# A fused two-block transformer layer on one core: modulation weights loaded first, two modulation blocks ahead of the squares of x, and the context normed during the Fourier projection

## The chip, the cores and the metric

The kernel runs on one core of a Trainium2 chip. The core has a matrix engine (TensorE, PE), a vector engine (VectorE, DVE), a scalar engine (ScalarE, ACT), a small general engine (GpSimd, POOL) and SyncE (SP), which here issues all DMAs in one queue. Each engine executes its own list of instructions in order and waits on semaphores that others raise. The metric is the time of the program on the device in microseconds (us), lower being better.

## The reference

A diffusion-style block with a context (depth 1) and then two layers of a second block. All data is float32, sequence 512, width 1024, context length 256. What matters here is the start:

```python
mod  = silu(c)     @ w_mod + b_mod          # c: one row; w_mod: 1024 x 6144
modc = silu(c_ctx) @ w_mod + b_mod
sh1, sc1, g1, sh2, sc2, g2 = split(mod, 6)  # the same for modc
h  = rms(x,  norm1) * (1 + sc1)  + sh1      # x:  512 x 1024
hc = rms(xc, norm1) * (1 + csc1) + csh1     # xc: 256 x 1024
P  = project(h)                             # h @ w_in: Fourier part, q, k, v, delta-rule inputs, gates
Pc = project(hc)                            # the context needs k, v, delta-rule inputs and gates, not the Fourier part
...                                         # attention, delta rule both ways, Fourier mix, w_out, MLP, then block 2 twice
```

rms(x, g) divides each row by the root of its mean square, and multiplies by g.

## The kernel before

Activations lie transposed: partition = channel within a tile of 128, free dimension = token. x is XT (8 tiles of 128 x 512), the context is XC (8 tiles of 128 x 256). A dense product takes its weights in pieces of 4 x 128 rows and 256 columns (512 KB, RAW). Each piece is split in two parts (SPL, "hi" by ACT at L1714, "lo" by DVE at L1998), and the product is made as three matmuls of parts (L1346); the activations are split likewise (HS for x, HC for the context, each with hi and lo). RAW and SPL have four slots.

The start of the program has these steps:

- SP issues the small constants, XT, XC, eight modulation pieces (MW, 512 KB each, into eight slots), the first four dense pieces (Fourier columns in two pieces, gates in a small one, and one more), small constants, and then, each when its slot has been used, modulation pieces 8 to 15.
- `mean_square` (L421): ACT squares a tile into one of three TMP slots, PE adds its column sums by a matmul with ones (L1381), DVE makes mean + eps (L2023), ACT the root (L1731), DVE the reciprocal (L2026). The result is R for x and RC for the context.
- `mod(j)` (L349): eight matmul groups over two pieces (L1361) make 256 columns of the modulation for c and c_ctx as a row; DVE copies it to MR (L2004, three buffers); two small matmuls turn it to columns (L1372); DVE adds the bias into MOD (L2008). mod(j) for j = 0 to 3 holds shifts, for 4 to 7 scales.
- After each pair of modulation blocks `gain` makes SCG = g (1 + scale), and `modulate` makes two tiles of HS: DVE x * SCG * R into TMP (L2041), ACT adds the shift and writes hi (L1735), DVE writes lo (L2046). `modulate` emits the DVE step of the next tile ahead of the lo step of the tile before it, if it is called for more than one tile.
- `split_first` stands in the plan ahead of the third pair: there ACT and DVE split the first four dense pieces (L1255 to L1264 of the planner).
- `dense(W["w_in"][0] ...)` is the Fourier projection (48 matmuls of 128 x 512), then come the gates (24 matmuls of 16 x 256 on HC, 24 of 16 x 512 on HS) and the projections that both x and the context need.

The order of each engine's list is that of the plan (`emit`). Work that is to lie beside dense matmuls is written as a generator in a list (`behind`, `aside`); `products` calls `tick` after each group of matmuls, and each tick lets each generator do one step. With rate 2 there are two ticks for each group. PSUM banks are handed out in turn (`single`, `pair`).

## Time and profile before

| | |
|---|---|
| time, median of 3 runs | 3332.59 us (3331.94 to 3334.54) |
| the profiled execution's own time | 3333.74 us |
| its span, first to last instruction | 3331.9 us |
| PE busy | 3178.4 us, 95% of the span |
| DVE, ACT busy | 1773.2 us (53%), 1112.9 us (33%) |
| mean granted TensorE clock | 0.969 |
| DMA | 288.19 MB, mean 86 GB/s |

The profile is of one execution. Its times are counted from the first instruction. PE is close to always busy after the first tenth, but not at the start: in the page's first slice of 83 us it is busy for seven tenths, with the granted clock at 0.8 of full speed, and the DMA queue moves 243 GB/s there against 86 on average. The granted clock has two levels, 0.50 (1.2 GHz) and 1.00 (2.4 GHz); a value between is a mean over a stretch. An instruction is shown with its line of the kernel, what it writes and reads, and, in brackets, how long its engine was idle in front of it and who ended the wait. A matmul in plain float32 is recorded as two, a matmul of split parts as one. The modulation weights appear as MW, and SP's own issue instructions as SPq.

### The profile page before, as it was taken

Reading aid. Unit: us, or ns where it says so; the run is one execution under the profiler, and the core shown is the slowest. Engines: PE = TensorE matmul, PEld = TensorE weight load, DVE = VectorE, ACT = ScalarE, POOL = GpSimd, SP = SyncE. Lnnn points to the kernel's source line nnn. Section 1 sums busy time; section 2 is a strip of 40 time slices with the busy share of each in tenths; the row PEclk is TensorE's granted clock in tenths of the full one; section 3 lists DMA queues with packets and bytes.
Section 4 is the critical chain, followed back from the end, with each engine's and each line's share of the span. In section 5 each row is a group of like instructions: output and inputs, shape, how many; then the busy total and the mean of one; then the engine's idle time right before and its main releaser. Section 6 shows DMA issues by size and latency. Waiting matters only on the chain.

```text
span 3331.9 us, 42705 instructions
## 1 busy us (share of the span) xinstructions
PE 3178.4 (95%) x17856; PEld 2509.2 (75%) x17856; DVE 1773.2 (53%) x2414; ACT 1112.9 (33%) x1574; POOL 63.3 (2%) x65
## 2 busy tenths in 40 slices
PE   7796889989999999999999999999999999999997
PEld 4564864578888888876788888888887767888886
DVE  4534554353435434587865434654345877643446
ACT  3321224342333322334443223432233254432233
POOL 0001410000000000000000000000000000000000
PEclk8897987999999999999999999999999999999999
DMA  6231000123222222221122322323222212223222
GB/s 243 93 119 51 4 32 1 38 77 101 95 95 101 95 95 98 91 99 45 64 101 90 101 96 91 104 100 97 99 88 88 89 45 89 89 101 97 93 91 73
DMA packets 81935, 288.19 MB, mean 86 GB/s; under 512 B 9552, under 2 KB 11344, under 8 KB 81360
## 3 DMA queue, kind: packets, MB, share of 16 engines
q1 hardware_dynamic: 81744, 285.46, 25.7%
q8 instruction: 142, 2.33, 0.3%
q14 instruction: 49, 0.40, 0.0%
HBM read 283.33 MB, written 2.10 MB: 86 GB/s over the span
## 4 chain that ended last, share of the span: by engine, by line
PE 90%; DVE 5%; issue 3%; ACT 1%; DMA 1%; POOL 0%; SPq 0%; DVEq 0%; ACTq 0%; POOLq 0%
PE PS L1346 77%; PE PS L1428 3%; PE PS L1663 1%; PE PS L1607 1%; PE PS L1627 1%; PE PS L1665 1%; PE PS L1361 1%; DVE XD L2114 1%; PE PS L1615 1%; PE PS L1684 1%; DMA MW<-in_w_mod 1%; PE PS L1673 1%; DVE SM L2290 1%; PE PS L1557 0%; ACT SPL L1714 0%
## 5 line engine op out<-in xcount | busy, mean ns | idle before, releaser
L1346 PE MATMUL PS<-HS,SPL 128*128 128x512 f32 (+1 forms) x7752 | 1804.9, 393 | 10.0 <-DVE HS L2046 7.3
L1346 PEld LDWEIGHTS PS<-HS,SPL 128*128 128x128 f32 (+1 forms) x7752 | 1455.2, 188 | 331.3 <-issue 20.7
L1998 DVE TENSOR_TENSOR SPL<-RAW,SPL 128x1024 fp32r<-128x1024 f32 (+1 forms) x491 | 584.2, 1193 | 722.5 <-ACT SPL L1714 718.8
L1714 ACT ACTIVATE SPL<-RAW 128x1024 fp32r<-128x1024 f32 (+1 forms) x491 | 503.2, 1028 | 843.7 <-PE PS L1346 843.4
L1346 PE MATMUL PS<-FF,SPL 128*128 128x512 f32 x2880 | 654.6, 389 | 0.0
L1346 PEld LDWEIGHTS PS<-FF,SPL 128*128 128x128 f32 x2880 | 540.6, 188 | 112.2
L2375 DVE SCALAR_TENSOR_TENSOR CA<-AP__137,CW,CA 128x512 f32<-128x512 f32 x240 | 180.1, 750 | 6.2
L1899 ACT ACTIVATE FF<-TMP 128x512 fp32r<-128x512 f32 x88 | 55.7, 633 | 235.1 <-DVE TMP L2345 235.1
L1893 ACT ACTIVATE SA<-SA 128x512 f32<-128x512 f32 x88 | 55.6, 633 | 191.4 <-DVE SA L2335 191.4
L2335 DVE TENSOR_TENSOR SA<-PS,R 128x512 f32<-128x512 f32 x88 | 60.5, 692 | 98.5 <-PE PS L1346 98.2
L2290 DVE TENSOR_REDUCE SM<-PS 128x1 f32<-128x768 f32 (+2 forms) x96 | 61.8, 644 | 87.3 <-PE PS L1608 50.3
L1842 ACT ACTIVATE PB<-PS,SM 128x768 f32<-128x768 f32 (+2 forms) x96 | 62.7, 653 | 110.1 <-DVE SM L2290 109.4
L2347 DVE TENSOR_TENSOR FF<-TMP,FF 128x512 fp32r<-128x512 f32 x88 | 61.0, 693 | 66.1 <-ACT FF L1899 66.1
L1346 PE MATMUL PS<-MS,SPL 128*128 128x512 f32 x384 | 88.0, 390 | 1.2 <-DVE MS L2460 1.2
L1346 PEld LDWEIGHTS PS<-MS,SPL 128*128 128x128 f32 x384 | 71.9, 188 | 16.9 <-DVE MS L2460 2.0
L2311 DVE SCALAR_TENSOR_TENSOR HS<-XT,VEC,HS 128x512 fp32r<-128x512 f32 x64 | 48.1, 752 | 55.8 <-ACT HS L1878 49.0
L2316 DVE SCALAR_TENSOR_TENSOR XT<-PS,XT 128x512 f32<-128x512 f32 x80 | 55.1, 689 | 40.0 <-PE PS L1346 40.0
L1878 ACT ACTIVATE HS<-XT,VEC 128x512 fp32r<-128x512 f32 x56 | 40.6, 724 | 96.1 <-DVE XT L2316 96.1
L2342 DVE TENSOR_TENSOR TMP<-PS,R 128x512 f32<-128x512 f32 x88 | 60.5, 688 | 21.6 <-PE PS L1346 21.6
L2345 DVE TENSOR_TENSOR TMP<-TMP,SA 128x512 f32<-128x512 f32 x88 | 60.9, 693 | 3.0
L1721 ACT ACTIVATE TMP<-XT 128x512 f32<-128x512 f32 x80 | 49.5, 619 | 33.6 <-DVE XT L2316 17.9
L2019 DVE TENSOR_TENSOR ACC<-ACC,TMP 128x512 f32<-128x512 f32 x76 | 52.2, 687 | 10.4 <-ACT TMP L1721 9.8
(289 smaller groups left out, 2258.6 us busy)
## 6 DMA issues: line engine op xcount, KB each, us to landing
RAW<-in_w_ff_in SPq DMA_DIRECT2D x176, 512.0 KB, 3.7
RAW<-in_w_in SPq DMA_DIRECT2D x88, 512.0 KB, 3.7
RAW<-in_w_ff_out SPq DMA_DIRECT2D x80, 512.0 KB, 3.5
RAW<-in_w_ff SPq DMA_DIRECT2D x64, 512.0 KB, 3.6
MW<-in_w_mod SPq DMA_DIRECT2D x48, 512.0 KB, 4.7
RAW<-in_w_out SPq DMA_DIRECT2D x24, 512.0 KB, 3.7
RAW<-in_w_ple_gate SPq DMA_DIRECT2D x16, 512.0 KB, 3.7
RAW<-in_w_ff_out SPq DMA_DIRECT2D x16, 256.0 KB, 2.7
```

The source lines that it names most:

```text
L1346: m = pe.matmul(o, w[x][:, k, rows], r.T[:, r.k0 + k, y, 0:r.cols], start=r.start and k == 0 and (x, y) == (0, 0), stop=r.stop and k == r. ...
L1428: m = pe.matmul(PS[hp, o.b, 64 * x:64 * x + 64], lhs[h][:, x, :], rhs[h][:, x, :] if len(rhs[h].shape) == 3 else rhs[h], start=True, stop= ...
L1714: a.activation(SPL[:, s, 0, 0:n], RAW[:, s, 0:n], AF.Copy).then_inc(w_hi, 1)
L1842: a.activation(s.row[:, 0:s.n], two_banks(s.uses, s.n), AF.Exp, bias=s.stat[:, 0:1], accum_out=s.stat[:, 1:2]).then_inc(free[s.uses[0].b], 1)
L1899: a.activation(FF[:, r.k, 0, :], TMP[:, r.slot, :], AF.Copy).then_inc(s_ffhi, 1)
L1998: v.tensor_tensor(SPL[:, s, 1, 0:n], RAW[:, s, 0:n], SPL[:, s, 0, 0:n], ALU.subtract).then_inc(w_lo, 1)
L2290: v.tensor_reduce(s.stat[:, 0:1], two_banks(s.uses, s.n), AX, ALU.max, negate=True).then_inc(s_mx, 1)
L2335: v.tensor_tensor(SA[:, r.sa, :], PS[:, r.use.b, :], R[:, :], ALU.mult).then_inc(free[r.use.b], 1)
L2342: v.tensor_tensor(t, PS[:, r.use.b, :], R[:, :], ALU.mult).then_inc(free[r.use.b], 1)
L2345: v.tensor_tensor(t, t, SA[:, r.sa, :], ALU.mult).then_inc(s_glu, 1)
L2347: v.tensor_tensor(FF[:, r.k, 1, :], t, FF[:, r.k, 0, :], ALU.subtract).then_inc(s_fflo, 1)
L2375: m = v.scalar_tensor_tensor(out=acc, in0=x, scalar=w, in1=acc, op0=ALU.mult, op1=ALU.add)
```

## The change

SP no longer issues XC directly behind XT. Behind XT come modulation pieces 0 to 7 and only the first dense piece; dense pieces 1 to 3, XC and the small constants are issued where modulation piece 7 has been used, behind the fetch of piece 15. The squares of x are emitted behind the first two modulation blocks. The squares of the context, RC and the eight HC tiles are a generator in `behind`, which runs during the Fourier projection, one `modulate` call for each tile. What is left of it behind the projection is drained there.

```diff
@@ -436,8 +436,6 @@
         give(u)
         return r.done
 
-    m_r = mean_square(XT, m_x, R[:, :], 512)
-    m_rc = mean_square(XC, m_xc, RC[:, :], 256)
 
     def gain(at, name, j, n, waits):
         r = Rec()
@@ -468,16 +466,39 @@
         if k < 4:
             mod(k)
             mod(4 + k)
-        else:
+        if k == 0:
+            m_r = mean_square(XT, m_x, R[:, :], 512)
+        if k == 4:
             tick()
         if k:
             i = 2 * k - 2
             gain(8, "n1", i, 2, [mod_mark[k - 1], mod_mark[3 + k]])
             hx_ready += modulate(HS, (i, i + 1), lambda j: XT[:, j, :], lambda j: SCG[:, j, 0:1],
                                  lambda j: MOD[:, j, 0:1], R[:, :], 512, [m_r])
-    hc_ready = modulate(HC, range(8), lambda j: XC[:, j, :], lambda j: SCG[:, j, 1:2], lambda j: MOD[:, j, 1:2],
-                        RC[:, :], 256, [m_rc])
     catch_up()
+    hc_ready = []
+
+    def context():
+        u = single()
+        for j in range(8):
+            r = Rec()
+            r.x, r.mark, r.use, r.j, r.n = XC[:, j, :], m_xc, u, j, 256
+            r.slot, r.after = tmp()
+            r.sq = count(s_sq)
+            slot_end[r.slot] = r.added = count(s_part) if j < 7 else u.mark
+            emit("square_sum", r)
+            if j % 2:
+                yield 1
+        r = Rec()
+        r.use, r.dst, r.n, r.width = u, RC[:, :], 256, 1024
+        r.root, m_rc = count(s_root), count(s_rms)
+        emit("root_of", r)
+        give(u)
+        for j in range(8):
+            hc_ready.extend(modulate(HC, (j,), lambda j: XC[:, j, :], lambda j: SCG[:, j, 1:2],
+                                     lambda j: MOD[:, j, 1:2], RC[:, :], 256, [m_rc]))
+            if j % 2:
+                yield 1
 
     ev_marks, qk_done = {}, {}
     apart.append(mods_apart(range(8, 24)))
@@ -493,7 +514,10 @@
         return ev
 
     rate[0] = 2
+    behind.append(context())
     dense(W["w_in"][0], 8, HS, hx_ready, evac_to(FT, 0, "f"))
+    while behind:
+        tick()
 
 
     m_tri = load("tri", TRI[:, :, :], D["c_tri"])
@@ -1286,15 +1310,9 @@
         sp.dma_start(ones[:, :], D["c_ones"]).then_inc(landed["ones"], 16)
         sp.dma_start(ident[:, :], D["c_ident"]).then_inc(landed["id"], 16)
         sp.dma_start(XT[:, :, :], D["xT"]).then_inc(landed["x"], 16)
-        sp.dma_start(XC[:, :, :], D["ctxT"]).then_inc(landed["xc"], 16)
         for p in mod_pieces[:8]:
             fetch_mod(p)
-        for p in pieces[:4]:
-            fetch(p)
-        sp.dma_start(onesbd[:, :], D["c_onesbd"]).then_inc(landed["bd"], 16)
-        sp.dma_start(idb[:, :], D["c_idb"]).then_inc(landed["idb"], 16)
-        sp.dma_start(causal[:, :], D["c_causal"]).then_inc(landed["causal"], 16)
-        sp.dma_start(madd[:, :, :], D["c_madd"]).then_inc(landed["madd"], 16)
+        fetch(pieces[0])
 
         def split(p):
             if p.i + 4 < len(pieces):
@@ -1306,6 +1324,14 @@
                 sp.wait_ge(*r.used)
                 fetch_mod(r.p.then)
             if r.p.i == 7:
+                fetch(pieces[1])
+                sp.dma_start(XC[:, :, :], D["ctxT"]).then_inc(landed["xc"], 16)
+                for p in pieces[2:4]:
+                    fetch(p)
+                sp.dma_start(onesbd[:, :], D["c_onesbd"]).then_inc(landed["bd"], 16)
+                sp.dma_start(idb[:, :], D["c_idb"]).then_inc(landed["idb"], 16)
+                sp.dma_start(causal[:, :], D["c_causal"]).then_inc(landed["causal"], 16)
+                sp.dma_start(madd[:, :, :], D["c_madd"]).then_inc(landed["madd"], 16)
                 for p in mod_pieces[16:18]:
                     fetch_mod(p)
```

SP's list at its start, before. MW_69 are the modulation slots of pieces 0 to 15, MW those of later pieces, RAW the dense weights (w_in, w_gates):

```order
4 L1288 DMA XT<-in_xT 128x4096
5 L1289 DMA XC<-in_ctxT 128x2048
6 L1283 DMA MW_69<-in_w_mod 128x1024 x8
7 L1280 DMA RAW<-in_w_in 128x1024 x2
8 L1280 DMA RAW<-in_w_gates 128x128
9 L1280 DMA RAW<-in_w_in 128x1024
10 L1294 DMA onesbd<-in_c_onesbd 128x128
11 L1295 DMA idb<-in_c_idb 128x128
12 L1296 DMA causal<-in_c_causal 128x128
13 L1297 DMA madd<-in_c_madd 128x128
14 L1283 DMA MW_69<-in_w_mod 128x1024 x8
15 L1283 DMA MW<-in_w_mod 128x1024 x2
```

And with the change:

```order
4 L1312 DMA XT<-in_xT 128x4096
5 L1307 DMA MW_69<-in_w_mod 128x1024 x8
6 L1304 DMA RAW<-in_w_in 128x1024
7 L1307 DMA MW_69<-in_w_mod 128x1024 x8
8 L1304 DMA RAW<-in_w_in 128x1024
9 L1328 DMA XC<-in_ctxT 128x2048
10 L1304 DMA RAW<-in_w_gates 128x128
11 L1304 DMA RAW<-in_w_in 128x1024
12 L1331 DMA onesbd<-in_c_onesbd 128x128
13 L1332 DMA idb<-in_c_idb 128x128
14 L1333 DMA causal<-in_c_causal 128x128
15 L1334 DMA madd<-in_c_madd 128x128
```

XC (128x2048) has moved from behind XT to behind all sixteen first modulation pieces and the second dense piece; three of the four dense pieces stand there too.

PE's list from its start, before. ones is the operand of the square sums, C_66 the conditioning columns, MR a modulation row:

```order
1 L1381 MATMUL PS<-TMP,ones 128x512 x8
2 L1381 MATMUL PS<-TMP,ones 128x256 x8
3 L1361 MATMUL PS<-MW_69,C_66 32x256 x12
4 L1372 MATMUL PS<-VEC,MR 128x2 x2
5 L1361 MATMUL PS<-MW_69,C_66 32x256 x8
6 L1372 MATMUL PS<-VEC,MR 128x2 x2
```

And with the change:

```order
1 L1387 MATMUL PS<-MW_69,C_66 32x256 x12
2 L1398 MATMUL PS<-VEC,MR 128x2 x2
3 L1387 MATMUL PS<-MW_69,C_66 32x256 x4
4 L1407 MATMUL PS<-TMP,ones 128x512 x8
5 L1387 MATMUL PS<-MW_69,C_66 32x256 x4
6 L1398 MATMUL PS<-VEC,MR 128x2 x2
7 L1387 MATMUL PS<-MW_69,C_66 32x256 x8
8 L1398 MATMUL PS<-VEC,MR 128x2 x2
```

Four modulation pieces (16 matmuls) now stand ahead of the squares of x (128x512 x8), and the context's squares (128x256 x8) are gone from there. In the Fourier projection PE's list with the change is as follows, where L1372 are dense matmuls and L1407 the context's squares:

```order
19 L1372 MATMUL PS<-HS,SPL 128x512 x12
20 L1407 MATMUL PS<-TMP,ones 128x256 x4
21 L1372 MATMUL PS<-HS,SPL 128x512 x12
22 L1387 MATMUL PS<-MW,C_66 32x256 x4
23 L1407 MATMUL PS<-TMP,ones 128x256 x4
24 L1372 MATMUL PS<-HS,SPL 128x512 x24
25 L1387 MATMUL PS<-MW,C_66 32x256 x4
26 L1372 MATMUL PS<-HC,SPL 16x256 x24
```

The context's squares stand between the dense matmuls of the first and second piece; before, nothing but the two modulation pieces stood there.

DVE's list for the context, before (L2041 is the first step of a tile, L2046 its lo part):

```order
35 L2041 SCALAR_TENSOR_TENSOR TMP<-XT,SCG,R 128x512 x2
36 L2046 SCALAR_TENSOR_TENSOR HS<-TMP,MOD,HS 128x512 x2
37 L2041 SCALAR_TENSOR_TENSOR TMP<-XC,SCG,RC 128x256 x2
38 L2046 SCALAR_TENSOR_TENSOR HC<-TMP,MOD,HC 128x256
39 L2041 SCALAR_TENSOR_TENSOR TMP<-XC,SCG,RC 128x256
40 L2046 SCALAR_TENSOR_TENSOR HC<-TMP,MOD,HC 128x256
41 L2041 SCALAR_TENSOR_TENSOR TMP<-XC,SCG,RC 128x256
42 L2046 SCALAR_TENSOR_TENSOR HC<-TMP,MOD,HC 128x256
```

And with the change (L2067 and L2072 are the same two steps, L2024 the split, L2049 and L2052 make RC):

```order
34 L2072 SCALAR_TENSOR_TENSOR HS<-TMP,MOD,HS 128x512 x2
35 L2024 TENSOR_TENSOR SPL<-RAW,SPL 128x1024
36 L2049 TENSOR_SCALAR RC<-PS 128x256
37 L2052 RECIPROCAL RC<-RC 128x256
38 L2067 SCALAR_TENSOR_TENSOR TMP<-XC,SCG,RC 128x256
39 L2072 SCALAR_TENSOR_TENSOR HC<-TMP,MOD,HC 128x256
40 L2067 SCALAR_TENSOR_TENSOR TMP<-XC,SCG,RC 128x256
41 L2072 SCALAR_TENSOR_TENSOR HC<-TMP,MOD,HC 128x256
42 L2067 SCALAR_TENSOR_TENSOR TMP<-XC,SCG,RC 128x256
43 L2072 SCALAR_TENSOR_TENSOR HC<-TMP,MOD,HC 128x256
44 L2067 SCALAR_TENSOR_TENSOR TMP<-XC,SCG,RC 128x256
```

The split of the fifth dense piece and RC stand ahead of the HC tiles, and the two steps of a tile follow each other, where before the next tile's first step stood between them. The first four splits stand where they stood: behind the first HS pair and ahead of the third modulation pair.

## Rows read from the trace of the kernel before

**Rows 1.** Page, section 4 (chain by engine) and two groups of section 5.
```profile
PE 90%; DVE 5%; issue 3%; ACT 1%; DMA 1%; POOL 0%; SPq 0%; DVEq 0%; ACTq 0%; POOLq 0%
...
L1998 DVE TENSOR_TENSOR SPL<-RAW,SPL 128x1024 fp32r<-128x1024 f32 (+1 forms) x491 | 584.2, 1193 | 722.5 <-ACT SPL L1714 718.8
L1714 ACT ACTIVATE SPL<-RAW 128x1024 fp32r<-128x1024 f32 (+1 forms) x491 | 503.2, 1028 | 843.7 <-PE PS L1346 843.4
```

**Rows 2.** All engines by stretch: busy us, granted clock, DMA share, GB/s.
```profile
0.00:10.00 10.00, 0.00 (x0) 0.00 (x0) 0.23 (x1) 1.50 (x2) 0.52 (x5) 1.00 0.79 287
10.00:20.00 10.00, 9.07 (x16) 3.81 (x16) 0.00 (x0) 6.10 (x9) 0.00 (x0) 1.00 1.00 386
36.00:47.00 11.00, 5.49 (x40) 3.03 (x40) 8.60 (x15) 4.79 (x7) 0.00 (x0) 0.65 1.02 414
```

**Rows 3.** Chain of waits, in order of time: start us, length us, what.
```profile
2.12 8.02 DMA XT<-in_xT
...
28.91 0.61 PE PS L1372 x4
29.51 0.61 PE PS L1361 x8
30.15 0.44 DVE MR L2004
...
34.01 0.16 DVE SCG L2031
```

**Rows 4.** Timeline of PE: start us, us, line op out<-in xcount [idle before].
```profile
10.93 9.34 PE L1381 MATMUL PS<-TMP,ones 128*128 128x512 f32 x16 [10.93 <-ACT TMP L1727]
22.11 3.76 PE L1381 MATMUL PS<-TMP,ones 128*128 128x256 f32 x16 [1.84 <-ACT TMP L1727]
...
41.51 1.01 PE L1372 MATMUL PS<-VEC,MR 128*128 128x2 f32 x4 [5.75 <-DVE MR L2004]
42.45 1.93 PE L1361 MATMUL PS<-MW,C 128*32 128x256 f32 x16
...
51.12 8.20 PE L1346 MATMUL PS<-HS,SPL 128*128 128x512 f32 x24
...
59.82 5.74 PE L1346 MATMUL PS<-HS,SPL 128*128 128x512 f32 x24
...
66.80 2.96 PE L1346 MATMUL PS<-HC,SPL 128*16 128x256 f32 x24 [0.66 <-issue]
```

**Rows 5.** Timeline of DVE.
```profile
21.70 3.35 DVE L2026 RECIPROCAL R<-R 128x512 f32<-128x512 f32 x1 [0.69 <-ACT R L1731]
...
37.35 3.70 DVE L1998 TENSOR_TENSOR SPL<-RAW,SPL 128x1024 fp32r<-128x1024 f32 x4 [0.19 <-ACT SPL L1714]
...
56.51 0.87 DVE L2041 SCALAR_TENSOR_TENSOR TMP<-XC,SCG,RC 128x256 f32<-128x256 f32 x2
...
61.93 0.48 DVE L2041 SCALAR_TENSOR_TENSOR TMP<-XC,SCG,RC 128x256 f32<-128x256 f32 x1
...
62.99 0.48 DVE L2046 SCALAR_TENSOR_TENSOR HC<-TMP,MOD,HC 128x256 fp32r<-128x256 f32 x1 [0.18 <-ACT HC L1735]
```

**Rows 6.** PE by stretch: length, busy us (x), granted clock, DMA share, GB/s.
```profile
25.00:36.00 11.00, 8.74 (x108) 1.00 0.89 301
36.00:39.00 3.00, 0.00 (x0) 1.00 1.03 414
42.00:56.00 14.00, 12.96 (x67) 0.50 0.40 158
88.00:94.00 6.00, 5.41 (x16) 0.50 0.00 0
304.00:309.00 5.00, 2.60 (x73) 1.00 0.00 0
309.00:310.00 1.00, 1.00 (x26) 0.50 0.00 0
```

**Rows 7.** Landing times of the modulation weights' DMAs up to 70 us.
```profile
DMA to landing us min/median/max: 3.7/8.6/16.4
```

## The prediction

> **What bounds the kernel now.** I read the page first. The chain that ended last is 90% TensorE (PE) [rows 1], and the change touches only the first 90 us, so the question is how many microseconds later or sooner PE gets through that stretch; everything behind it waits on PE, VectorE (DVE) and ScalarE (ACT) and moves along with it. Then I read the stretch in stages, in the order in which the prediction uses them.
>
> The DMA queue is full from the start: 287 GB/s in the first 10 us, 386 in the next, 414 from 36 to 47 [rows 2]. x lands at 10.14 [rows 3]. PE then does the squares of x, 10.93 to 20.27, and those of the context, 22.11 to 25.87 [rows 4]. R is finished by DVE at 25.05 and RC at 28.57 (25.87 plus 2.70; its reciprocal is the 1.75 in front of the first copy of a modulation row) [rows 5]. Rounds of PE and DVE follow [rows 3], and then DVE reaches the four splits of w_in, 37.35 to 41.05 [rows 5]. From their end it takes 10.07 us to the first dense matmul at 51.12 [rows 4]; I call that start t0. While DVE splits PE is idle, 5.75 us [rows 4], and its granted clock falls: 1.00 (2.4 GHz) at 36 to 39, 0.50 (1.2 GHz) from 42 to 56 [rows 6]. The Fourier projection's 24+24 matmuls end at about 65.6, the gates' matmuls on HC run 66.80 to 69.76 [rows 4]: HC was complete at 63.47 [rows 5], so PE hardly waits for it. The last HC triplet ends 69.76-51.12 = 18.6 us after t0.
>
> **Front: where t0 goes.** The change takes the context's 1.05 MB and 1.3 MB of dense weights and constants from ahead of the last eight modulation pieces. But the split of the first four dense pieces keeps its place on DVE, ahead of the third modulation pair, and it needs pieces 1, 2 and 3, which now are asked for only behind modulation piece 15, with the context between them. So I work out both arrivals.
>
> DVE's arrival at the splits. Four modulation pieces must now land and be used before the squares of x. Bytes up to piece 3: 0.30 of vectors, 2.10 of x, 4x0.524, together 4.50 MB; x landed when 2.87 MB had moved against 2.40 of its own, so 0.47 more are in flight: 4.97 MB, at 386 GB/s from 2.87 at 10 us: 15.4 us. Its matmuls, at the lower clock about 1.0 us: 16.4. Squares of x 9.34 [rows 4] (I take that their first third runs at half the pace of the rest, as now: the modulation matmuls ahead of them are no help, since the same mix from 42 on, 1.93 us for two pieces, did not raise the clock before the dense matmuls had run for 5 us [rows 4, 6]): 25.7. To R finished 25.05-20.27 = 4.78: 30.5. DVE has been shut behind that reciprocal; then MR 0.44, PE 0.61 for the columns and 0.61 for piece 7, MR 0.44 [rows 3], and 0.2 for the handovers: 32.8. From SCG to the splits 37.35-34.01 = 3.34 [rows 3, 5]: 36.1, which is 1.2 before today's. So of the 6.5 us from 22.11 to 28.57 that the context takes on the chain, the wait for four pieces ahead of the squares of x gives back most.
>
> Arrival of the weights. Piece 15 may be fetched when piece 7 is used, which stands behind the MR copy: 32.3. A 512 KB piece needs at least 3.7 us to land [rows 7]: 36.1. Behind it dense piece 1, the context, the gates' weights and dense piece 3, 0.524+1.049+0.066+0.524 = 2.16 MB at 414 GB/s: 5.2, so 41.3. ACT's half of the split 1.03, DVE's 1.19 [rows 1], two handovers of 0.1: 43.7 against 41.05 (the gates' piece fits in between). Behind the waiting splits on DVE stand the MR copies of the third pair, and PE waits for these. t0 is **2.7 us later**. Bounds: had the queue never paused, the 13.47 MB up to dense piece 3 and 0.4 in flight would be through at 10+11.0/0.40 = 37.5, and the splits end at 39.9, t0 1.2 earlier; with 1.5 us more for the small constants or a slower landing it is 4.2 later. I take 2.7, since the refetch of a slot needs PE's use of it, and that is in the order.
> The queue here moves 414 GB/s [rows 2]. The Trainium skill (DMA: Bandwidth & Descriptors, Where 436 GB/s comes from) gives about 358 GB/s as what HBM grants one core. By it even the unbroken stream would end at 40.7 and the early case would vanish; the row of this case decides.
>
> **Context beside the Fourier projection.** Counted from t0. First 12 matmuls at the lower clock 5.1 (12 of the 24 in 8.20; the other 12 take 3.1) [rows 4]. Four squares of the context: half of 3.76, so 1.9; ACT can make them in time, since DVE is done with HS at 56.51, +5.4 [rows 5], and ACT before it. 12 matmuls 3.1, a modulation piece 0.6, four squares 1.9: +12.6. RC 2.7, handover 0.1: +15.4. Then the eight HC tiles. Today DVE issues the next TMP before it asks ACT for the last tile, and a tile costs 0.77 (56.51 to 61.93, seven steps) [rows 5]. The new loop calls modulate for one tile at a time, and the order shows TMP, HC, TMP, HC in strict turn. One tile alone is TMP at 61.93, ACT, then HC from 62.99 to 63.47: 1.54, and as DVE starts the next instruction 0.08 before the one in front ends, 1.46. Eight tiles 11.7, one MR copy between them 0.35: HC is complete at +27.4, its last three matmuls end at +27.8.
> PE meanwhile: second half of the projection 5.7 and a modulation piece 0.6 [rows 4], so it stands at the gates' matmuls at +18.9 and waits there, doing three matmuls (0.37) for each tile. **27.8-18.6 = 9.2 us lost**. Of it 3.8 is the squares, which now lie on PE inside the projection, the rest is the wait. Bounds: 3.8 if the tiles ran at today's 0.77 after all (5.4 less than 9.2), 10.7 if the first squares still meet the lower clock. I take 9.2, from the order.
> The FT copies and the next split on ACT now stand behind the eight HC activations; ACT is through with HC at about +26.9; two FT copies of 0.6, the split's 1.03 and 1.19 on DVE end at +30.9. PE needs that split behind the gates' 24 matmuls on x (512 columns, 5.7 like the half projection), at +33.5, so these hide it; without them it would add 3 us. POOL's pad memsets wait for the last HC tile too; nothing needs them before XD's sums.
>
> **Clock.** From +18.9 to +27.8 PE is busy about a quarter of the time. At 304 to 309 it was busy 2.60 of 5 us and the clock fell right behind, 0.50 at 309 [rows 6]. So I expect a fall during the wait, and the stretch 88 to 94 [rows 6] shows what one costs: some 5.4 us of PE's work at half speed, **2.6 us** lost. Bounds 0 (it holds) and 7.1 (24 gates' matmuls of 16 columns all at 0.43 instead of 0.24, 4.5, and another 2.6 behind them). I take the ordinary stretch.
> The Trainium skill (TensorE: Matmul & The Clock Gate, A second HAM failure mode) says that frequent short idles between groups of matmuls can make the clock swing. The stretch before 309 bears it out; by it the 2.6 stand, without it the sum is the second rival's.
>
> **Sum.** 2.7+9.2+2.6 = 14.5 us on the profiled execution's 3333.74 (span 3331.9): 3348.2. That execution lies 1.15 above the median of the runs, so I predict **3347 us**.
>
> **Rivals.**
> 1. The clock holds in the wait. For it: from 25 to 36 PE had gap after gap and kept 1.00. Against: PE was busy 8.74 of those 11 us [rows 6]; here it would be a quarter. 2.7+9.2 = 11.9, 3344.5.
> 2. The clock falls and the thin gates' matmuls do not raise it. For it: from 42 on PE was busy with small matmuls nearly throughout, at 0.50 [rows 6]. Against: 16x512 streams without pause. 2.7+9.2+7.1 = 19.0, 3351.5.
> 3. The queue keeps up and t0 is 1.2 early. For: the bytes. Against: the refetch waits for PE. -1.2+9.2+2.6, 3343.
> 4. Not slower: in front of the third pair PE's idle is so short that its clock never falls. Needs dense pieces 1 to 3 there when DVE comes, at 33.8 if the squares of x run warm (2.5 sooner): splits end at 37.5, t0 3.5 early; and the upper clock from there saves 3.8 on the small matmuls (four column groups 1.01 against 0.61, five pieces 0.97 against 0.54) and 2.2 on the first 12 dense ones [rows 3, 4]. -9.5+9.2+2.6, 3335. It decides if PE's idle there ends while the clock is still up, as it is at 36 to 39 [rows 6]; today the idle is 5.75 [rows 4]. Against it: the byte count, which puts the weights at 37.5 at best.
>
> That the context isn't hidden, as the change has it, is the main case itself.
>
> **Chances.** Forecast 0.42, rival 1 0.18, rival 2 0.18, rival 3 0.16, rival 4 0.06. Range: the outer ends 3343 and 3351.5 widened by the bounds of t0, 3341 to 3353. What a measurement of this kernel tells from no change is about 0.2%, 6.7 us: only rival 4 (3335) falls inside it, with a little of rival 3. Faster 0.01, same 0.07, slower 0.92.
>
> **What would show it.** Splits on DVE ending at 42 to 45; XC squares inside the projection; HC tiles 1.46 apart; gates' HC matmuls stretched from 3 us to about 9, with PE idle waiting for DVE's HC; granted clock 0.50 behind. HC tiles 0.8 apart, or splits ending before 39, would break the sum; a shift at 84 us (the gate chain on ACT) that is smaller than at 70 would mean that a later wait takes some of it up.

## The result, and the profile after

| | before | after |
|---|---|---|
| median | 3333.57 us (3331.94 to 3336.30, 4 runs) | 3353.41 us (3352.90 to 3355.47, 4 runs) |
| profiled execution, span | 3333.74, 3331.9 | 3353.65, 3351.8 |

The ratio is 1.0059, 95% interval 1.0047 to 1.0071: slower, by about 20 us, where 14.5 on the profiled execution had been forecast. The time lies 0.4 us above the upper end of the range.

The page shows the same kind of program (compare [rows 1]): the chain is still PE's, and the splits of the weights and the matmuls take what they took.

```profile
PE 89%; DVE 5%; issue 3%; ACT 2%; DMA 1%; POOL 0%; SPq 0%; DVEq 0%; ACTq 0%; POOLq 0%
...
L2024 DVE TENSOR_TENSOR SPL<-RAW,SPL 128x1024 fp32r<-128x1024 f32 (+1 forms) x491 | 584.3, 1193 | 737.1 <-ACT SPL L1740 733.3
L1740 ACT ACTIVATE SPL<-RAW 128x1024 fp32r<-128x1024 f32 (+1 forms) x491 | 503.3, 1028 | 847.2 <-PE PS L1372 841.7
```

So nearly all of the 20 us must come from the first 110 us, and the table of marks below has 18.84 of it there. This is PE's timeline there (start us, us, line op out<-in xcount, and the idle before it), to be held against [rows 4]:

```profile
11.72 2.29 PE L1387 MATMUL PS<-MW,C 128*32 128x256 f32 x16 [11.72 <-DMA MW<-in_w_mod]
...
17.23 9.25 PE L1407 MATMUL PS<-TMP,ones 128*128 128x512 f32 x16
...
31.66 0.94 PE L1398 MATMUL PS<-VEC,MR 128*128 128x2 f32 x4 [3.07 <-DVE MR L2030]
...
46.79 1.02 PE L1398 MATMUL PS<-VEC,MR 128*128 128x2 f32 x4 [9.52 <-DVE MR L2030]
...
58.71 4.75 PE L1372 MATMUL PS<-HS,SPL 128*128 128x512 f32 x12 [2.16 <-issue]
63.29 1.93 PE L1407 MATMUL PS<-TMP,ones 128*128 128x256 f32 x8
...
76.48 0.52 PE L1372 MATMUL PS<-HC,SPL 128*16 128x256 f32 x3
77.57 0.52 PE L1372 MATMUL PS<-HC,SPL 128*16 128x256 f32 x3 [0.56 <-DVE HC L2072]
79.02 0.52 PE L1372 MATMUL PS<-HC,SPL 128*16 128x256 f32 x3 [0.93 <-DVE HC L2072]
80.48 0.82 PE L1372 MATMUL PS<-HC,SPL 128*16 128x256 f32 x3 [0.94 <-DVE HC L2072]
...
86.64 0.82 PE L1372 MATMUL PS<-HC,SPL 128*16 128x256 f32 x3 [0.64 <-DVE HC L2072]
87.25 6.88 PE L1372 MATMUL PS<-HS,SPL 128*16 128x512 f32 x24
```

Four things stand out. The idle in front of the third modulation pair has grown from 5.75 to 9.52 us. The first dense matmul (t0) has a wait of 2.16 of its own, which it did not have before, and comes at 58.71 instead of 51.12. The gates' matmuls on HC go in threes, each waiting for its tile. And there is a wait of 3.07 at 28.6, in which PE has nothing to do while DVE makes R.

The long idle is best read in the chain of waits (start us, us, what); before, the same stretch had no DMA in it:

```profile
31.66 0.94 PE PS L1398 x4
32.60 1.05 PE PS L1387 x8
...
33.67 0.33 SPq L1307
...
34.04 0.43 SPq L1304
...
34.52 1.20 SPq L1328
...
35.75 0.43 SPq L1304
...
36.23 7.77 DMA RAW<-in_w_in
...
44.02 1.06 ACT SPL L1740
```

SP gets to modulation piece 15 at 33.67, spends 2.56 us on asking for what stands between, asks for dense piece 3 at 36.23, and it lands at 44.00. Ahead of that request the chain is PE's: column matmuls and modulation piece 7 take 0.94 and 1.05 at the lower clock, where before they took 0.61 and 0.61 [rows 3]. DVE's four splits, a single group of 3.70 us in [rows 5], are now apart (the third, of the small gates' piece, starts at 43.01 and takes 0.29):

```profile
37.43 1.23 DVE L2024 TENSOR_TENSOR SPL<-RAW,SPL 128x1024 fp32r<-128x1024 f32 x1 [0.20 <-ACT SPL L1740]
41.02 1.23 DVE L2024 TENSOR_TENSOR SPL<-RAW,SPL 128x1024 fp32r<-128x1024 f32 x1 [2.37 <-ACT SPL L1740]
...
45.11 1.22 DVE L2024 TENSOR_TENSOR SPL<-RAW,SPL 128x1024 fp32r<-128x1024 f32 x1 [1.80 <-ACT SPL L1740]
```

PE by stretch (length, busy us (x), granted clock, DMA share, GB/s), for [rows 2, 6]:

```profile
26.00:32.00 6.00, 2.93 (x32) 0.98 0.53 172
32.00:44.00 12.00, 5.27 (x39) 0.50 0.89 313
44.00:62.00 18.00, 12.01 (x64) 0.50 0.40 160
64.00:79.00 15.00, 13.53 (x72) 1.00 0.29 95
82.00:88.00 6.00, 3.83 (x14) 0.50 0.01 1
90.00:100.00 10.00, 10.00 (x106) 1.00 0.43 149
```

The clock is down from 32 on; before it was still at 1.00 from 36 to 39 [rows 6]. And from 26 to 32 the queue moves 172 GB/s, less than half of what it can: SP stands at requests that need a slot PE has not yet used (it waits for PE seven times, 23.3 us in all, up to 60).

Marks in the two timelines, in us:

| | before | after | shift |
|---|---|---|---|
| last of the first four splits ends | 41.05 | 46.33 | +5.28 |
| from there to t0 | 10.07 | 12.38 | +2.31 |
| from t0 to the gates' matmuls on x | 18.48 | 28.54 | +10.06 |
| from there to the matmuls with TRI | 18.99 | 20.18 | +1.19 |
| matmuls with TRI | 88.59 | 107.43 | +18.84 |
| profiled execution | 3333.74 | 3353.65 | +19.91 |

The last 1.07 us come later. Behind the gate chain the clock in after is 0.54 from 134 to 136, where before it was 1.00 at the same work (114 to 116). The matmuls on XD there take longer, and the next matmuls on HC start at 141.72 instead of 120.88: the shift has grown to 20.84, of which 0.93 is gone by the end. No experiment was made on that.

### The profile page after: what moved, and what is told of

Its sections match the earlier page's. It is cut to its first block, busy times and chain, and to the rows that moved or that the text cites. A ratio compares the mean times of both kernels' runs of the same rounds, so it can differ in the third digit from the quotient of the medians.

```text
span 3351.8 us, 42704 instructions
## 1 busy us (share of the span) xinstructions
PE 3187.6 (95%) x17856; PEld 2510.6 (75%) x17856; DVE 1773.3 (53%) x2414; ACT 1112.8 (33%) x1574; POOL 63.2 (2%) x65
## 4 chain that ended last, share of the span: by engine, by line
PE 89%; DVE 5%; issue 3%; ACT 2%; DMA 1%; POOL 0%; SPq 0%; DVEq 0%; ACTq 0%; POOLq 0%
PE PS L1372 76%; PE PS L1454 3%; PE PS L1689 1%; DMA MW<-in_w_mod 1%; PE PS L1633 1%; PE PS L1653 1%; PE PS L1387 1%; PE PS L1691 1%; DVE XD L2140 1%; PE PS L1641 1%; PE PS L1710 1%; PE PS L1699 1%; DVE SM L2316 1%; ACT SPL L1740 0%; PE PS L1583 0%
## 5 line engine op out<-in xcount | busy, mean ns | idle before, releaser
L1372 PE MATMUL PS<-HS,SPL 128*128 128x512 f32 (+1 forms) x7752 | 1805.4, 393 | 12.2 <-DVE HS L2072 7.3
L1372 PEld LDWEIGHTS PS<-HS,SPL 128*128 128x128 f32 (+1 forms) x7752 | 1454.5, 188 | 334.0 <-issue 24.3
L2024 DVE TENSOR_TENSOR SPL<-RAW,SPL 128x1024 fp32r<-128x1024 f32 (+1 forms) x491 | 584.3, 1193 | 737.1 <-ACT SPL L1740 733.3
L1372 PE MATMUL PS<-FF,SPL 128*128 128x512 f32 x2880 | 654.6, 389 | 0.0
L1372 PEld LDWEIGHTS PS<-FF,SPL 128*128 128x128 f32 x2880 | 540.5, 188 | 112.3
L1372 PE MATMUL PS<-MS,SPL 128*128 128x512 f32 x384 | 88.0, 390 | 1.2 <-DVE MS L2486 1.2
L1372 PEld LDWEIGHTS PS<-MS,SPL 128*128 128x128 f32 x384 | 71.9, 188 | 16.9 <-DVE MS L2486 2.0
L1387 PE MATMUL PS<-MW,C 128*32 128x256 f32 x384 | 38.4, 491 | 23.5 <-DMA MW<-in_w_mod 23.4
```

What stands on the lines that cost most here:

```text
L1372: m = pe.matmul(o, w[x][:, k, rows], r.T[:, r.k0 + k, y, 0:r.cols], start=r.start and k == 0 and (x, y) == (0, 0), stop=r.stop and k == r. ...
L1387: m = pe.matmul(PS[32 * k:32 * k + 32, r.use.b, 0:256], C32[:, r.k0 + k, :], r.p.buf[:, 256 * k:256 * k + 256], start=r.k0 == 0, stop=r.k0 ...
L2024: v.tensor_tensor(SPL[:, s, 1, 0:n], RAW[:, s, 0:n], SPL[:, s, 0, 0:n], ALU.subtract).then_inc(w_lo, 1)
```

## Experiments

Besides before and after, twelve kernels ran, in three groups, each group on one chip with its own runs of the kernel before, to which its ratios belong.

| kernel | median us | ratio to before (95%) | splits end | t0 | TRI |
|---|---|---|---|---|---|
| before | 3333.0 to 3334.1 | 1 | 41.05 | 51.12 | 88.59 |
| after | 3353.41 | 1.0059 (1.0047, 1.0071) | 46.33 | 58.71 | 107.43 |
| a1_bank | 3352.83 | 1.0057 (1.0042, 1.0072) | 48.16 | 58.22 | 107.85 |
| a2_pairs | 3349.09 | 1.0046 (1.0030, 1.0063) | 44.55 | 56.92 | 101.34 |
| a3_weights | 3348.33 | 1.0044 (1.0029, 1.0059) | 41.03 | 53.41 | 101.59 |
| a4_all | 3340.21 | 1.0017 (1.0008, 1.0027) | 40.75 | 50.82 | 94.02 |
| a5_swap | 3352.09 | 1.0055 (1.0040, 1.0070) | 47.13 | 59.51 | 105.39 |
| b1_ctx | 3347.65 | 1.0038 (1.0025, 1.0051) | 40.15 | 50.23 | 100.37 |
| b2_mods | 3338.00 | 1.0010 (1.0001, 1.0020) | 46.33 | 56.41 | 93.88 |
| b3_late | 3340.88 | 1.0016 (1.0007, 1.0025) | 46.76 | 56.84 | 93.17 |
| c1_front | 3329.93 | 0.9988 (0.9979, 0.9997) | moved | 45.51 | 83.51 |
| c3_rc | 3330.01 | 0.9989 (0.9981, 0.9998) | moved | 46.65 | 83.39 |
| c4_mods | 3327.65 | 0.9984 (0.9976, 0.9993) | moved | 44.56 | 80.61 |
| d1_fill | 3345.45 | 1.0034 (1.0021, 1.0048) | 37.99 | 48.05 | 98.34 |

The marks are of one profiled execution each. They say more than the times where a wait of 2 us is at stake, since the runs of one kernel spread over 3 to 10 us.

### a1_bank: another PSUM bank for the last modulation column

Why does the first dense matmul wait 2.16 us with "issue" as its releaser? PE's list of after, with what each row waits for, tells it:

```
48 L1398 MATMUL PS<-VEC_63,MR_67 128x2 [waits bank0_taken,bank6_taken]
49 L1398 MATMUL PS<-VEC_63,MR_67 128x2
50 L1372 MATMUL PS<-HS_50,SPL_52 128x512 [waits mod_lo,bank0_taken,w_lo]
```

Before, the row that answers to the first one has bank1_taken and bank7_taken: the last column went to bank 1. The context's squares used to take one bank ahead of the modulation; without them the whole turn is one bank earlier, and the last column lies in bank 0, where the Fourier projection starts. DVE frees it with the MOD step, and that stands behind the HS tiles of the third pair:

```profile
55.58 1.41 DVE L2067 SCALAR_TENSOR_TENSOR TMP<-XT,SCG,R 128x512 f32<-128x512 f32 x2
57.12 1.42 DVE L2072 SCALAR_TENSOR_TENSOR HS<-TMP,MOD,HS 128x512 fp32r<-128x512 f32 x2
58.45 0.15 DVE L2034 TENSOR_TENSOR MOD<-PS,VEC 128x4 f32<-128x4 f32 x1
```

58.45 plus 0.15 and the handover is t0. The edit skips one bank:

```diff
     hx_ready = []
+    turn[1] += 1
     for k in range(5):
```

> The changed kernel with the turn of the PSUM banks moved on by one, so that the last modulation column lies in bank 1 as before and not in bank 0, which the first dense matmul needs. In the trace of the changed kernel PE stands idle from 56.5 to 58.7 ahead of the first dense matmul, and DVE writes the last modulation column out of its bank at 58.45 to 58.60. Theory (bank turn): the first dense matmul starts at about 56.5, 2.2 us sooner; the squares of the context are then held a little by ACT, so 1.5 to 2.2 us are kept: about 3351.5 us. Rival (PE waited for the activations or the split weights): the start stays at 58.7 and the time at 3353.4.

Measured 3352.83. The wait is gone: from the end of the splits to t0 it takes 10.06 us, as before the change, not 12.38. In the time little of it shows: 0.6 us between the medians, with a spread of 5 us. In the profiled execution the dense pieces landed later, with the same order of requests (ACT's timeline):

```profile
41.76 1.06 ACT L1741 ACTIVATE SPL<-RAW 128x1024 fp32r<-128x1024 f32 x1 [4.52 <-DMA RAW<-in_w_in]
```

In after the same step starts at 39.94. Dense piece 1 was asked for at 33.88 there and at 34.04 in after. The cause of the wait is shown by this run; its worth is read at the marks, here and in a4_all (12.38 to 10.06 and 10.07).

### a2_pairs: the next context tile's first step ahead of the last tile's lo

```diff
-            hc_ready.extend(modulate(HC, (j,), ...))
+            emit("modulate", r)            # tile j
+            if last:
+                emit("modulate_lo", last)  # tile j - 1
```

> The changed kernel with the next HC tile's first step on DVE issued ahead of the lo step of the tile before, as before the change; nothing else. Theory (strict turn): tiles come 0.8 us apart and not 1.46, HC is complete 5 us sooner, the gates' matmuls on x start at about 81.7 and not 87.3, and the granted clock falls later or not at all, worth 1 more: about 3347 us. Rival (the tiles are late because the squares and RC are late, and ACT sets their pace): tiles stay over 1.2 us apart, less than 2 us gained, 3351.5 or more.

Measured 3349.09, and the tiles come every 0.8 us where DVE does nothing else:

```profile
77.96 0.52 PE L1385 MATMUL PS<-HC,SPL 128*16 128x256 f32 x3 [0.59 <-DVE HC L2085]
78.75 0.52 PE L1385 MATMUL PS<-HC,SPL 128*16 128x256 f32 x3 [0.28 <-DVE HC L2085]
```

From t0 to the gates' matmuls on x it takes 24.70 instead of 28.54: the strict turn of TMP and HC is worth 3.84 us. The bank wait of 2.16 is still there. That the splits end 1.78 sooner than in after isn't the edit's work: in this execution the clock came up earlier, and the squares of x took 7.13 instead of 9.25.

### a3_weights: dense pieces 1 to 3 requested right behind piece 0

```diff
-        fetch(pieces[0])
+        for p in pieces[:4]:
+            fetch(p)
```

with the three later requests dropped. The context and the constants stay late.

> The changed kernel with dense pieces 1 to 3 requested right behind piece 0, ahead of modulation pieces 8 to 15; the context and the constants stay late. Theory (late weights): DVE reaches the splits at 37.4 as now and is through with them at 41.1 and not 46.3; all behind it comes 5.2 us sooner: about 3348.2 us. Rival (the queue is what counts, order in it is indifferent): modulation pieces 8 to 15 then land 2.7 us later and hold PE and DVE, so 2.5 us or less is gained, 3351 or more.

Measured 3348.33. The splits end at 41.03, within 0.02 of the kernel before, and t0 comes 5.30 us sooner than in after. So the whole delay of the splits is the late weights. It also shows what the move of the squares is worth by itself: DVE is not at the splits any sooner than before, although the context is no longer in its way.

### a4_all: the three together

> The three repairs together: bank turn, HC tiles overlapped, dense pieces 1 to 3 early. What is left of the change is two modulation blocks ahead of the squares of x, the context loaded late, and its squares and RC inside the Fourier projection. Theory (three separate costs): their gains add up, 2+6.5+5.2 = 13.7 us, about 3339.7 us, still some 6 us over the kernel before, of which 3.8 are the context's squares on PE inside the projection. Rival (they hide one another): the sum falls short by more than 3 us, 3343 or more.

Measured 3340.21: 13.2 us less than after, where 13.7 had been expected, so the three costs add up. t0 is at 50.82 (before 51.12), with no wait in front of it. From t0 to the gates' matmuls on x 24.21, 5.73 more than before, and at TRI 5.43 more; in the time 5.7 by the ratio. That is the part of the change that the three edits leave in: the context's squares on PE inside the projection, and RC and eight tiles behind them. Against a3_weights t0 is 2.59 sooner, 2.31 of it between the end of the splits and t0, which is the bank.

### a5_swap: the gates' x part ahead of the context's

```diff
-    products(W["w_gates"], 8, [(HC, 256, us[:1], hc_ready), (HS, 512, us[1:], None)], 16)
+    products(W["w_gates"], 8, [(HS, 512, us[1:], None), (HC, 256, us[:1], hc_ready)], 16)
```

> The changed kernel with the gates' matmuls in the other order: the 24 on x first, then the 24 on the context. Theory (PE waits for the last HC tiles): at 76.5 PE goes on with the x part, 5.7 us at the upper clock, and only then waits; the context part ends at about 87.1, where the changed kernel has both parts done at 94.1. 7 us sooner, about 3346.5 us. Rival (the matmuls on the context are late but something else behind them sets the pace, the splits on ACT and DVE that stand behind the HC tiles): the next dense matmuls start later than 2 us behind the last gates' matmul, less than 4 us gained.

Measured 3352.09: 1.3 us of the 7 expected. At the marks it is 2.84 from t0 to TRI (45.88 instead of 48.72). PE should have filled the wait with the x part at 77.98. It did not:

```profile
71.57 5.84 PE L1372 MATMUL PS<-HS,SPL 128*128 128x512 f32 x24
...
82.32 6.98 PE L1372 MATMUL PS<-HS,SPL 128*16 128x512 f32 x24 [4.34 <-DVE MR L2030]
89.13 2.97 PE L1372 MATMUL PS<-HC,SPL 128*16 128x256 f32 x24
```

The x part writes to a bank that still holds a modulation row, and DVE's copy of that row (81.75) stands behind four context tiles. In after the row's copy stands at 80.34, behind four context tiles too, and the x part comes only at 87.25: the same wait was there, hidden behind the wait for HC.

### b1_ctx: the context's part alone, on the kernel before

The squares, root and tiles of the context as the generator of the change, everything else as before (loads too), with the bank skipped as in a1_bank.

> The kernel before with one part of the change alone: squares of the context, RC and the HC tiles as a generator during the Fourier projection, one tile at a time; loads and modulation blocks as before (and the PSUM turn moved on by one, so that the first dense matmul doesn't meet the last column's bank). Theory: the front gets 3.4 us shorter (first modulation row copied at 25.1 and not 28.5, splits end at 37.7, first dense matmul at 47.7), then 9.3 to 10 us are lost on squares and tiles, and 1 to 2 on the clock: 3333+7.5, about 3340.5 us. Rival (the context's work is hidden by the projection, as the idea of it is): the front's 3.4 us are kept, 3330 us.

Measured 3347.65; I had expected about 3340.5. The stretch behind t0 costs 10.98 us (29.46 against 18.48), where it costs 10.06 in after. The gain in front did not come: with 3.7 us of squares less on PE the splits end only 0.9 sooner. Here is why:

```profile
19.95 1.50 PE L1385 MATMUL PS<-MW,C 128*32 128x256 f32 x24
25.14 0.87 PE L1396 MATMUL PS<-VEC,MR 128*128 128x2 f32 x4 [3.68 <-DVE MR L2028]
25.94 1.93 PE L1385 MATMUL PS<-MW,C 128*32 128x256 f32 x16
27.80 1.01 PE L1396 MATMUL PS<-VEC,MR 128*128 128x2 f32 x4
28.74 1.93 PE L1385 MATMUL PS<-MW,C 128*32 128x256 f32 x16
```

PE waits 3.68 us for DVE, which is making R, and the clock behind it is 0.50. A round of column matmuls and two pieces then takes 2.80 us. Before it took 1.72 (28.91 to 30.63), since the context's squares lay in that wait. The Trainium skill (TensorE: Matmul & The Clock Gate, HAM oscillation) says that a wait for DMA between groups of matmuls can take the clock down, so that the next group starts cold. Here the wait is for DVE, and this trace agrees: the granted clock is 0.94 from 20 to 26 and 0.50 from 26 to 32.

### d1_fill: is it the clock? Four idle matmuls into b1_ctx's wait

```diff
+            if r.p.i == 2:
+                for _ in range(4):
+                    pe.matmul(PS[:, r.use.b, :], ones[:, :], XT[:, 0, :], start=True, stop=True)
```

> b1_ctx with four extra 128x512 matmuls of ones by x ahead of modulation piece 2, into the bank that the piece's first matmul overwrites; their sums are not used. They stand in the stretch (21.45 to 25.14) in which TensorE in b1_ctx had nothing to do. Theory (the context's squares kept the clock up there, and without them the modulation rounds run at half clock, 2.8 us in place of 1.72): the granted clock stays at full in 22 to 32, the rounds take 1.7 to 1.8 us, VectorE's splits end 2 to 2.5 us sooner than b1_ctx's 40.15 and the time is 3345 (3343 to 3346.5), against 3347.1 to 3347.7 of b1_ctx. Rival (the rounds follow the landing of their pieces, the clock there costs nothing): splits end at 40.1, 3347 to 3348.

```profile
21.65 3.70 PE L1386 MATMUL PS<-XT,ones 128*128 128x512 f32 x8
...
25.85 0.61 PE L1399 MATMUL PS<-VEC,MR 128*128 128x2 f32 x4
...
27.57 0.61 PE L1399 MATMUL PS<-VEC,MR 128*128 128x2 f32 x4
```

Work of no use, 3.70 us of it, makes the front faster: the granted clock is 1.00 from 26 to 32, the rounds are 1.72 again, the splits end at 37.99 instead of 40.15, t0 is 2.18 sooner and TRI 2.03. The rival (the rounds follow the landing of their pieces) is out. The time doesn't resolve it: the medians, 3345.45 and 3347.65, are of two chips, by the ratios it is 1.3 us with intervals that overlap (1.0034 and 1.0038), and the profiled execution of d1_fill is 1.29 us longer than that of b1_ctx.

### b2_mods: the modulation blocks' part alone, on the kernel before

Two modulation blocks ahead of both squares, loads as before.

> The kernel before with one part alone: two modulation blocks ahead of the squares of x and of the context; the context stays loaded behind x. Theory (the squares are held by the fourth modulation piece): that piece lands at about 18, squares of x end at 28.4, R and RC at about 35, the first dense matmul about 3 us later than before: 3336 us. Rival (the two blocks are out of the way earlier and pay for it): within 1 us of before.

Measured 3338.00: +5.29 at the splits, at t0 and at TRI alike, and 3.3 in the time by the ratio (3.9 between the medians). Its profiled execution, 3342.42, was the slowest of its ten. Nothing is gained by having the blocks early, for PE has to wait for their pieces (they land behind the context here) while x is already there:

```profile
13.95 2.27 PE L1362 MATMUL PS<-MW,C 128*32 128x256 f32 x16 [13.95 <-DMA MW<-in_w_mod]
...
19.53 9.41 PE L1382 MATMUL PS<-TMP,ones 128*128 128x512 f32 x16
```

Before, the squares start at 10.93 [rows 4].

### b3_late: the late weights alone, on the kernel before

```diff
-        for p in pieces[:4]:
-            fetch(p)
+        fetch(pieces[0])
...
+                for p in pieces[1:4]:
+                    fetch(p)
```

The second fetch stands behind that of modulation piece 15.

> The kernel before with dense pieces 1 to 3 requested behind modulation piece 15; everything else as before. Theory (the splits wait for the weights): splits end at 41.6 to 43, 1 to 2 us late, 3334 to 3335 us; the cost in the changed kernel is greater because there piece 15 is asked for later and the context lies in between. Rival (order in the queue is free as long as all is moved by 42): splits end at 41.1, no change.

Measured 3340.88, splits +5.71, t0 +5.72, TRI +4.58 (1.14 comes back in the projection's first half, which meets the lower clock for a shorter time), where I had expected 1 to 2 us. The pieces were asked for from 33.75 on, the first of them landed at about 42.9, over 9 us later, and ACT stood still:

```profile
42.97 1.25 ACT L1715 ACTIVATE SPL<-RAW 128x1024 fp32r<-128x1024 f32 x2 [5.86 <-DMA RAW<-in_w_in]
```

Together with a3_weights this shows the term from both sides: the splits end 5.3 us sooner when it is taken out of after, 5.7 later when it is put into before.

### c1_front: a better front

If DVE's row ahead of t0 is what counts, both the splits and RC's reciprocal can leave it. The context's squares stay where they were, in R's wait; its root comes only ahead of the context's tiles; and the splits of dense pieces 0 and 1 go between the two modulation blocks of the third and the fourth pair, where DVE waits for PE anyway.

```diff
         if k < 4:
             mod(k)
+            if k >= 2:
+                emit("split_first", k - 1)
             mod(4 + k)
```

> Kernel before with its loads and its squares as they are, but the context's root is taken only ahead of the context's modulations, and VectorE's splits of dense weight pieces 0 and 1 stand between the two modulation blocks of k = 2 and k = 3, pieces 2 and 3 at the first dense matmul. Theory (the time of this kernel is set by the row of VectorE's work ahead of the first dense matmul, and the clock holds because the context's squares still stand beside R's root): before, the four splits (37.35 to 41.05) and RC's reciprocal stand in front of the last two modulation rows. With both off that row the first dense matmul comes at 43 to 44 instead of 51.12; the context's tiles are then ready late again (a wait of about 2 to 3 us for HC), so 5 to 8 us are gained: 3326 (3322 to 3330). Rival A (the landing of the last modulation pieces sets it, VectorE's row does not): first dense matmul not before 49, gain at most 2 us: 3332. Rival B (everything gained in the front is lost at the context's wait and in a clock that falls in it): 3333.

Measured 3329.93, ratio 0.9988 (0.9979 to 0.9997), t0 at 45.51. Faster than before, by 4 us, less than the 7 expected. The order works, the clock does not stay up, and the bank's turn bites again:

```profile
35.89 1.01 PE L1384 MATMUL PS<-VEC,MR 128*128 128x2 f32 x4 [1.86 <-DVE MR L2016]
...
45.51 4.75 PE L1358 MATMUL PS<-HS,SPL 128*128 128x512 f32 x12
51.36 3.02 PE L1358 MATMUL PS<-HS,SPL 128*128 128x512 f32 x12 [1.11 <-DVE RC L2035]
```

At 35.89 an idle of 1.86 us was enough for the column matmuls to take 1.01 instead of 0.61. At 51.36 the projection's next tile wants the bank that holds the context's sum, and DVE reads that only at 50.89, with RC's first step.

### c3_rc: c1_front with RC made in the fourth pair

> As c1_front, with the context's root and reciprocal already in k = 3, behind VectorE's split of piece 1. Theory: the reciprocal then costs VectorE about 1.5 us beside landing or copies, and the context's modulations can start behind the last HS tile at once: the wait for HC of c1_front (2 to 3 us) goes, first dense matmul 0 to 1.5 us later: 3324.5 (3321 to 3329), 0.5 to 2.5 us below c1_front. Rival (the reciprocal stands in the row ahead of the last modulation row and moves the first dense matmul by all it takes, and nothing was waiting for HC): 1 to 2 us above c1_front.

Measured 3330.01. The wait of 1.11 is gone, but t0 comes 1.14 later, because PE now waits 1.97 for RC's first step in front of a column. At TRI it is 0.12 ahead of c1_front: a draw, neither the gain of the theory nor the loss of the rival.

### c4_mods: c3_rc with modulation blocks 0 and 4 between the two squares

> As c3_rc, with modulation blocks 0 and 4 ahead of the context's squares (behind the squares of x). This is the second part of the change in its cheap form: one pair only, no squares moved behind the weights' landing. Theory: pieces 8 to 11 of the modulation's weights are asked for 1 to 2 us sooner, the two row copies stand right behind R's reciprocal at 25 us, and the squares of the context cover the wait for them, so the first dense matmul comes 1 to 3 us before c3_rc's: 3322.5 (3318 to 3327). Rival (weights have not landed by 20 us and SBUF's readers are in strict turn, so squares wait behind modulation matmuls that wait for their pieces, and RC comes late): 1 to 3 us above c3_rc.

```profile
19.41 1.93 PE L1379 MATMUL PS<-MW,C 128*32 128x256 f32 x32
21.32 3.76 PE L1399 MATMUL PS<-TMP,ones 128*128 128x256 f32 x16
...
31.24 1.00 PE L1379 MATMUL PS<-MW,C 128*32 128x256 f32 x8 [1.19 <-DMA MW<-in_w_mod]
```

Measured 3327.65, ratio 0.9984 (0.9976 to 0.9993), t0 at 44.56, TRI at 80.61. That is 8.0 us ahead of before at TRI, 7.8 between the two profiled executions, and 5.3 by the ratio. It beats both kernels, but less than the 3322.5 (3318 to 3327) that I had expected. The larger part of the gain is c1_front's and c3_rc's, the splits off DVE's row ahead of t0. What the early blocks add is t0 2.09 sooner than in c3_rc, within the 1 to 3 expected, and 2.4 us between the medians. PE is busy without a gap from 14 to 26: modulation matmuls early, but only once x's squares are done, and the context's squares where PE has nothing else. Then PE waits for two modulation pieces (1.19 and 0.28 us), and the clock, 1.00 from 26 to 30, is 0.50 from 31.6 on.

## Why the prediction was wrong

The direction and the two places were right, the sum was 5.4 us short (14.5 against 19.91): 4.9 too little for t0, 0.9 too little for the context, 1.1 behind TRI that the sum had no term for, and 1.4 too much for the clock. Step by step:

**Front, weights: the step that failed.** "t0 is 2.7 us later" was 7.59. Two causes. The splits ended 5.28 later, not 2.7. Of the 2.6 that were missing, 1.4 is that piece 15 was asked for at 33.67 and not 32.3, and 1.3 that from there dense piece 3 needed 10.33 us and not 9.0: SP's own requests took 2.56 in between, which the prediction counted at nothing, and the landing took longer than bytes over 414 GB/s (from 33.67 to 44.00 the queue moved 318 GB/s). The 10.33 is no unlucky draw: in the three other kernels with the same order of requests, a1_bank, a2_pairs and a5_swap, this stretch took 12.30, 11.87 and 11.76. a3_weights and b3_late show the whole term; no run parts SP's requests from the landing.

**Front, bank turn: missed.** The remaining 2.31 us. That it takes 10.07 us from the end of the splits to t0 held for DVE's and PE's work, but the prediction never asked which bank the last column gets when one `single()` in front is gone. a1_bank and a4_all show it: 10.06 and 10.07 with the bank skipped. In the order it could be read beforehand from what the first dense matmul and the last column wait for. The Trainium skill (Perfetto Trace Analysis, Optimizing Tensor Performance, Matmuls) advises to rotate independent groups through the banks so that reading one out lies beside the next group; here all eight were in rotation and it still cost 2.2 us, since the turn came round to a bank whose reader stood behind 2.9 us of other work.

**Front, DVE's arrival: wrong, and it delayed the weights.** The prediction had DVE at the splits at 36.1, "which is 1.2 before today's". It came at 37.43, 0.08 later than before. R was finished at 31.25 instead of 30.5, and then the column matmuls and modulation piece 7 took 1.99 instead of 1.22, since PE's clock had fallen in the wait for R (3.07 us, then 0.50 from 32 on). The prediction saw that wait, but not the fall. b1_ctx and d1_fill show the mechanism and its price at t0, 2.2 us, where no other wait covers it. In after the late weights cover what it does to DVE's arrival, but piece 15 may be asked for only when piece 7 is used, so the two delays make up the 1.4 that its request came late.

**Context beside the projection: right.** 9.2 forecast, 10.06 measured; tiles at 74.51, 75.97, 77.43, 78.89 are 1.46 apart as forecast. a2_pairs gives 3.84 of it to the strict turn of the two steps, where the forecast had 5.4: the tiles themselves take 7.3 us there instead of 12.1, 4.8 less, and 0.9 of that goes into the projection's first matmuls, which met the lower clock for longer (their context tiles start 16.7 behind t0, not 15.8). Squares in the projection and RC, with the tiles as they came before, are 5.7 (a4_all).

**Clock in the wait for HC: right in kind, half the size.** It fell at about 80, as forecast, and was back at 90. The gates' x part took 6.88 instead of 5.71, 1.2 us, and 2.6 had been taken. Rival 2's number, 3351.5, is nearer to the result than the forecast's, but its mechanism isn't what happened: the x part did raise the clock, 1.00 from 90 on. (That without a fall "the sum is the second rival's" is a slip in the prediction; it is the first's, 11.9.) A number that comes near by the wrong term is no evidence for the term.

**The rivals.** 3 (the queue keeps up) fell by its own "against": 172 GB/s from 26 to 32, because refetches wait for PE. 4 (not slower) needed the weights at 37.5; they came at 44.

**Do the parts add up?** b1_ctx alone moves TRI by 11.78 and b2_mods alone by 5.29; with the bank's 2.3, which neither has, that is 19.4 against 18.84. The agreement is luck. b3_late alone moves TRI by another 4.58, and a3_weights, which has after's early blocks but not its late weights, ends the splits at 41.03 (41.05 before): in after the early blocks and the moved squares together cost nothing at that mark. In b2_mods the blocks do, for there the context is loaded ahead of their pieces (first modulation matmul at 13.95, in after 11.72) and its squares still stand behind those of x. What puts t0 late in after is the late weights and the bank.

## What to carry to other kernels

When work is taken away from the start of a kernel, ask three things of what is left: which engine was kept busy by it (its clock may fall in the hole, as in b1_ctx), which rotation it took a turn of (a buffer or bank that is handed out in turn shifts for everything behind), and which requests were queued ahead of it. A weight request that is moved behind requests that wait for slots cost here not its bytes but the whole wait for those slots, the issuing of what stood between, and a landing of 6 to 9.5 us in a loaded queue. And a wait that one edit uncovers was often there before: list the waits in order of their ends, not only the one that shows (a5_swap, c1_front, c3_rc).

## What the runs showed that I had not expected

- **Useless matmuls can pay.** 3.70 us of sums that nobody reads, put into a wait, brought the first dense matmul 2.2 us forward, as they kept the granted clock at 1.00 (2.4 GHz) for the short groups behind.
- **An idle of 1.86 us stood in front of a fall** (c1_front, up to 35.89), and those of 3.07 and 3.68 in after and b1_ctx did. In the kernel before, one of 1.60 passed without a fall, 1.00 from 25 to 36 [rows 6]. The length of the idle alone doesn't tell: in c4_mods one of 1.19 (up to 31.24) stood in front of a fall. The row of before is:

```profile
28.91 0.61 PE L1372 MATMUL PS<-VEC,MR 128*128 128x2 f32 x4 [1.60 <-DVE MR L2004]
```

- **Landing times scatter where the order doesn't.** Dense piece 1, behind the same requests, was on ACT 5.9 us after its request in after, 7.9 in a1_bank, 7.4 in a5_swap and 7.5 in a2_pairs. A gain of 2 us can drown in that, as a1_bank's did, so the parts of such a sum should be read at marks in the trace, between two events that the landing doesn't touch.
